# Small experts' up rows turned by plain transposes instead of half-merging products, and their second projections issued in one piece

## Chip, cores and metric

One core of a Trainium2 chip runs the whole program. The time is device microseconds of one launch; lower is better.

## What is computed

A two-layer decoder trunk on 256 tokens of width 1024: a retention layer with a dense SwiGLU, then a block-sparse attention layer with an eight-expert SwiGLU in which each token takes its top two experts. The change touches the expert part alone:

```python
def swiglu(x, w_in, w_out):
    gate, up = jnp.split(x @ w_in, 2, axis=-1)
    return (jax.nn.silu(gate) * up) @ w_out

def moe_swiglu(x, router, w_in, w_out):
    ...
    for e in range(N_EXPERTS):
        out = out + gates[:, e:e + 1].astype(x.dtype) * swiglu(xt, w_in[e], w_out[e])
```

Each expert has `w_in` of 1024 x 7168 and `w_out` of 3584 x 1024, all float32. The weights are read once.

## The kernel before

**Precision.** Matmuls run on 32-bit "fp32r" operands. Each weight tile is split in two parts, `whi` (a ScalarE copy that rounds, L894) and `wlo` (VectorE: the raw weights minus `whi`, L1056); each activation tile has such a pair as well. A product is then a sum of two or three matmuls.

**Units.** The expert weights come as units of 1 MB (128 x 2048). There are 8 jobs (one for each expert, sorted by how many tokens they have), each of 42 units. Four jobs are *big* (up to 128 tokens, three matmuls for each of four pieces: 12 matmuls of 512 columns for a unit, L1534 to L1536) and four are *small* (up to 64 tokens; the hi and lo halves of the 64 tokens lie side by side in the 128 columns of one stationary operand, so two matmuls for each piece: 8 for a unit, L1968 and L1969). Because of that, the result of a small gate or up product has 128 rows, 64 of the hi part and 64 of the lo part, and the two halves must still be added.

**Rings.** SyncE loads raw units into 8 buffers (`raw`, `more_raw`); a load is issued when the `wlo` of the unit eight places before is done. The split tiles `whi`/`wlo` have 4 buffers. In iteration n of its loop ScalarE writes `whi` of unit n + 4, for which it waits until TensorE has used unit n; VectorE then writes `wlo` of unit n + 4, and TensorE waits for that before unit n + 4.

**Order.** The order of the units is written out by hand in `STREAM`. A big and a small job run as a pair, in four blocks of the hidden dimension (4, 4, 4 and 2 units for each part). I call the place of a unit in its block, counted from the block's first unit (the big gate), its *offset*. Before, blocks 1 and 2 run: big gate (offsets 0 to 3), two units of small out of the block before (4, 5), big up (6 to 9), the other two of small out (10, 11), small gate (12 to 15), big out (16 to 19), small up (20 to 23). Block 0 of the second to fourth pair is the same with one and one unit of small out (22 units in all); block 3 has big gate 2, big up 2, small out 4, small gate 2, small up 2, big out 2. A pair is 84 units.

**Side work.** All of it is placed by unit number through tables such as `MUL_AT`, and lies between units in each engine's loop: of the big job, silu (ScalarE), times up (VectorE, L1424), transposes (TensorE, L1932), hi and lo of the turned rows (ScalarE L909, VectorE). Of the small job: ScalarE copies the gate rows to `rows4` (L918), TensorE turns them with eight 128 x 128 transposes (L2016), ScalarE copies the one half (L949), VectorE adds the other (L1452), ScalarE takes silu (L955). The up rows are copied too (L925), but they are turned by `turn_merged`: a product with `merge` (128 x 64, the sum of the identity's two halves), which turns the rows and adds the halves at once (L2006). VectorE multiplies straight from PSUM (L1458), ScalarE writes hi (L961), VectorE lo. Besides, four times in a pair a finished job's rows are split (`y_hi`, `y_lo`) and scattered by TensorE (L1902, L1903) and added to `h` (VectorE, L1415), and in the blocks of the first three pairs the next pair's tokens are gathered (L1871, copies L980 and L981).

Of the kernel before, what the change touches and what calls it, by code (L numbers as in the profile page):

```python
# [29 lines left out]
def build(nc, x, ln_g, ln_b, ret_w_in, ret_gn_g, ret_gn_b, ret_w_out, kv_w, moba_w_q, moba_w_out,  # L30
# [56 lines left out]
    for pair in range(JOBS // 2):  # L87
        for b in range(LAST + 1):
            big, small = 2 * pair, 2 * pair + 1
            end = pair == JOBS // 2 - 1 and b == LAST  # L90
            START[big, b] = len(STREAM)
            small_out = units_of(small, "out", b - 1) if b else units_of(small - 2, "out", LAST) if pair else []
            mid = len(small_out) // 2
            if b < LAST:
                STREAM += units_of(big, "gate", b) + small_out[:mid] + units_of(big, "up", b) + small_out[mid:]
                START[small, b] = len(STREAM)
                STREAM += units_of(small, "gate", b) + units_of(big, "out", b) + units_of(small, "up", b)
            else:
                STREAM += units_of(big, "gate", b) + units_of(big, "up", b) + small_out[:mid if end else None]
                START[small, b] = len(STREAM)  # L100
                STREAM += units_of(small, "gate", b) + units_of(small, "up", b) + units_of(big, "out", b)
            if end:
                STREAM += small_out[mid:] + units_of(small, "out", b)
# [23 lines left out]
    SEL_AT = {START[j - j % 2, 2] + 1 + 2 * (j % 2): j for j in range(JOBS)}  # L127
# [30 lines left out]
    with ctx:  # L158
# [59 lines left out]
        merge, _ = place("merge", [P, HALF])  # L218
# [33 lines left out]
        rows4, _ = place("rows4", [P, W], at=act4_at)  # L252
        act_small, _ = place("act_small", [P, BANK], at=past_at)
# [120 lines left out]
        gate_summed = sem("gate_summed")  # L374
        small_silu = sem("small_silu")
# [120 lines left out]
        def turned_gate():  # L496
            return ps[:, 0:2, :].rearrange("p a (c s n) -> p (a c) s n", s=2, n=HALF)
# [98 lines left out]
        def _(pool):  # L596
# [54 lines left out]
            pool.tensor_tensor(merge[:, :], ident[:, 0:HALF], ident[:, HALF:P], ALU.add).then_inc(moe_tables, 1)  # L651
# [7 lines left out]
            pool.wait_ge(moe_tables, 8)  # L659
# [24 lines left out]
        def _(act):  # L684
# [255 lines left out]

            def small_drains(n):

                if n in GATE_TURN_AT:
                    j, b = GATE_TURN_AT[n]
                    c = 2 * BLOCK_UNITS[b]
                    act.wait_ge(gate_turned, blocks(j, b))
                    if blocks(j, b) > 1:
                        act.wait_ge(small_lo, blocks(j, b) - 1)
                    nc.scalar.activation(act_small[:, 0:c * HALF].rearrange("p (c n) -> p c n", c=c),  # L949
                                         turned_gate()[:, 0:c, 1, :], ACT.Copy).then_inc(gate_half, 1)  # L950
# [42 lines left out]
            for n in range(MOE_UNITS):  # L993
# [4 lines left out]
                if n in SEL_AT:  # L998
                    copy_selT(SEL_AT[n], 3)
# [46 lines left out]
        def _(dve):  # L1046
# [316 lines left out]
            def sort_experts():  # L1363

                dve.wait_ge(counted, 1)
                dve.wait_ge(moe_tables, 9)
# [71 lines left out]
            def small_drains(n):  # L1438
# [8 lines left out]
                if n in GATE_SUM_AT:  # L1447
                    j, b = GATE_SUM_AT[n]
                    c = 2 * BLOCK_UNITS[b]
                    rows = act_small[:, 0:c * HALF].rearrange("p (c n) -> p c n", c=c)  # L1450
                    dve.wait_ge(gate_half, blocks(j, b))
                    nc.vector.tensor_tensor(rows, rows, turned_gate()[:, 0:c, 0, :], ALU.add).then_inc(gate_summed, 1)  # L1452
                if n in SMALL_MUL_AT:
                    j, b = SMALL_MUL_AT[n]
                    w = BLOCK_UNITS[b] * P
                    dve.wait_ge(small_silu, blocks(j, b))
                    dve.wait_ge(up_turned, blocks(j, b))
                    nc.vector.tensor_tensor(act_small[:, 0:w], act_small[:, 0:w], ps[:, 2, 0:w],  # L1458
# [72 lines left out]
        def _(pe):  # L1531
# [404 lines left out]
            def big_unit(n):  # L1936
# [10 lines left out]
                if q == 0 and part == "up" and blocks(j, b) > 1:  # L1947
                    pe.wait_ge(small_mul, blocks(j, b) - 1)
                    pe.wait_ge(up_copied, 7 * (j // 2) + 2 * b)
                    if b == 2:  # L1950
                        pe.wait_ge(selT_ready, j + 2)
# [19 lines left out]
            def small_unit(n):  # L1971
# [3 lines left out]
                if q == 0 and part == "gate":  # L1975
                    pe.wait_ge(big_silu, halves(j, b))
                    if b == 0:
# [25 lines left out]
            def turn_merged(rows, at, chunks):  # L2003

                for c in range(chunks):
                    last = pe.matmul(ps[:, at, c * HALF:(c + 1) * HALF], rows[:, c * P:(c + 1) * P], merge[:, :],  # L2006
                                     start=True, stop=True)
                return last

            def small_turn(n):  # L2010

                if n in GATE_TURN_AT:
                    j, b = GATE_TURN_AT[n]
                    pe.wait_ge(gate_copied, halves(j, b))
                    for c in range(2 * BLOCK_UNITS[b]):
                        last = pe.transpose(ps[:, c // 4, c % 4 * P:(c % 4 + 1) * P], rows4[:, c * P:(c + 1) * P], ident[:, :])  # L2016
                    last.then_inc(gate_turned, 1)
                if n in UP_TURN_AT:
                    j, b = UP_TURN_AT[n]
                    pe.wait_ge(up_copied, halves(j, b))  # L2020
                    turn_merged(rows4, 2, 2 * BLOCK_UNITS[b]).then_inc(up_turned, 1)
# [11 lines left out]
            pe.wait_ge(moe_tables, 9)  # L2033

            for n in range(MOE_UNITS):
# [19 lines left out]
                if n in SEL_AT:  # L2055
                    j = SEL_AT[n]
                    if SMALL[j]:
                        pe.wait_ge(selT_ready, j)
                    else:
                        pe.wait_ge(up_copied, 7 * (j // 2) + 4)  # L2060
                    turn_sel(sel_of(j), 3)
# [59 lines left out]
```

## Time and profile before

| what | value |
|---|---|
| three runs | 1403.58, 1406.47, 1406.56 us; median 1406.47 |
| the profiled execution | 1405.33 us, span of its records 1403.5 us |
| TensorE busy | 1371.3 us (98%) |
| VectorE busy | 1137.5 us (81%); in the expert part nearly all the time |
| ScalarE busy | 960.7 us (68%) |
| HBM read | 444.63 MB, 318 GB/s over the span |

The expert part runs from about 530 us to the end. Times in the trace are microseconds from the span's start; PE is TensorE, DVE VectorE, ACT ScalarE, SP SyncE. A duration is that of one instruction; where instructions overlap, the distance from one start to the next is shorter than the duration.

### The profile page before, as it was taken

To read this page: it belongs to the slowest core of one execution; us is meant where nothing else is said; L and a number is where in the kernel's file an instruction comes from. 1 tells how busy PE (TensorE), PEld (TensorE's weight loads), DVE (VectorE), ACT (ScalarE), POOL (GpSimd) and SP (SyncE) were. 2 spreads that over 40 slices of the span, in tenths; PEclk is the share of its full clock that TensorE was granted. 3 is DMA by queue.
4 is the path that set the end of the run, shared out by engine and by line. 5 is a ranking of instruction groups with operands and counts; after the bars stand their busy time and mean duration, and the time that the engine had idled before them with its cause. 6 is when DMAs were issued, how large, how long until landed. Compare 5 with 4: busy or idle time off the path is not lost.

```text
span 1403.5 us, 18365 instructions
## 1 busy us (share of the span) xinstructions
PE 1371.3 (98%) x7282; PEld 1172.3 (84%) x7282; DVE 1137.5 (81%) x807; ACT 960.7 (68%) x814; POOL 62.4 (4%) x64
## 2 busy tenths in 40 slices
PE   9999999999999999999999999999999999999996
PEld 9987788999979888788888788888788888788884
DVE  5455655444475668999999999999999999999997
ACT  5334444333454448788897888897888887888884
POOL 1001200000000003001100001200000000000000
PEclk9999999999999999999999999999999999999998
DMA  9654546555545437999999999999999999999992
GB/s 357 233 165 161 195 162 223 186 179 182 191 168 196 142 112 286 400 405 420 414 416 421 398 415 414 412 416 420 394 419 418 411 414 420 407 404 420 419 414 105
DMA packets 158742, 446.87 MB, mean 318 GB/s; under 512 B 7088, under 2 KB 46000, under 8 KB 158656
## 3 DMA queue, kind: packets, MB, share of 16 engines
q1 hardware_dynamic: 156832, 439.38, 80.9%
q0 software_dynamic: 1824, 6.33, 1.3%
q8 instruction: 56, 0.92, 0.2%
q14 instruction: 30, 0.25, 0.0%
HBM read 444.63 MB, written 1.05 MB: 318 GB/s over the span
## 4 chain that ended last, share of the span: by engine, by line
PE 81%; DVE 14%; ACT 2%; issue 2%; POOL 0%; DVEq 0%; ACTq 0%; POOLq 0%
PE ps L1534 20%; PE ps L1536 19%; PE ps L1535 19%; PE ps L1968 7%; PE ps L1969 7%; DVE wlo L1056 6%; DVE wlo_more L1056 3%; PE ps L2006 2%; PE ps L1871 1%; ACT whi L894 1%; DVE h L1415 1%; PE ps L1580 1%; PE ps L2016 1%; DVE wlo L431 1%; DVE act L1424 1%
## 5 line engine op out<-in xcount | busy, mean ns | idle before, releaser
L1056 DVE TENSOR_TENSOR wlo<-raw,whi 128x2048 fp32r<-128x2048 f32 (+1 forms) x214 | 478.8, 2256 | 16.8 <-ACT whi L894 16.6
L894 ACT ACTIVATE whi<-raw 128x2048 fp32r<-128x2048 f32 x208 | 395.3, 1916 | 69.6 <-PE ps L1536 66.0
L431 DVE TENSOR_TENSOR wlo<-raw,whi 128x2048 fp32r<-128x2048 f32 x80 | 183.5, 2294 | 155.2 <-ACT whi L424 155.2
L424 ACT ACTIVATE whi<-raw 128x2048 fp32r<-128x2048 f32 x82 | 156.8, 1912 | 153.3 <-PE ps L1536 150.4
L1534 PE MATMUL ps<-xT_hi,whi 128*128 128x256 f32 x576 | 163.4, 284 | 0.0
L1536 PE MATMUL ps<-xT_hi,wlo 128*128 128x256 f32 x576 | 163.0, 283 | 0.0
L1535 PE MATMUL ps<-xT_lo,whi 128*128 128x256 f32 x576 | 163.0, 283 | 0.0
L1534 PE MATMUL ps<-whi,xg_big 128*128 128x512 f32 x336 | 133.6, 398 | 2.0 <-DVE wlo L1056 2.0
L1968 PE MATMUL ps<-whi,xg_small 128*128 128x512 f32 x336 | 133.3, 397 | 0.0
L1536 PE MATMUL ps<-whi,xg_big 128*128 128x512 f32 x336 | 131.8, 392 | 0.0
L1535 PE MATMUL ps<-wlo,xg_big 128*128 128x512 f32 x336 | 131.4, 391 | 0.0
L1969 PE MATMUL ps<-wlo,xg_small 128*128 128x512 f32 x336 | 131.2, 391 | 0.0
L1534 PEld LDWEIGHTS ps<-xT_hi,whi 128*128 128x128 f32 x576 | 110.5, 192 | 0.5
L1535 PEld LDWEIGHTS ps<-xT_lo,whi 128*128 128x128 f32 x576 | 110.5, 192 | 0.4
L1536 PEld LDWEIGHTS ps<-xT_hi,wlo 128*128 128x128 f32 x576 | 110.5, 192 | 0.0
L1056 DVE TENSOR_TENSOR wlo_more<-raw,whi_more 128x2048 fp32r<-128x2048 f32 x42 | 96.0, 2285 | 3.2 <-ACT whi_more L894 3.2
L1056 DVE TENSOR_TENSOR wlo_more<-more_raw,whi_more 128x2048 fp32r<-128x2048 f32 x42 | 96.0, 2285 | 3.0 <-ACT whi_more L894 3.0
L1056 DVE TENSOR_TENSOR wlo<-more_raw,whi 128x2048 fp32r<-128x2048 f32 x42 | 96.0, 2286 | 2.7 <-ACT whi L894 2.7
L894 ACT ACTIVATE whi_more<-raw 128x2048 fp32r<-128x2048 f32 x42 | 80.6, 1920 | 10.7 <-PE ps L1536 10.7
L894 ACT ACTIVATE whi_more<-more_raw 128x2048 fp32r<-128x2048 f32 x42 | 80.6, 1920 | 10.5 <-PE ps L1536 10.5
L1534 PE MATMUL ps<-whi,xT_hi 128*128 128x512 f32 (+1 forms) x224 | 85.2, 380 | 2.4 <-DVE wlo L431 2.2
L894 ACT ACTIVATE whi<-more_raw 128x2048 fp32r<-128x2048 f32 x42 | 80.5, 1917 | 10.2 <-PE ps L1536 10.2
(273 smaller groups left out, 2686.4 us busy)
## 6 DMA issues: line engine op xcount, KB each, us to landing
raw<-in_moe_w_in SPq DMA_DIRECT2D x167, 1024.0 KB, 8.0
raw<-in_moe_w_out SPq DMA_DIRECT2D x85, 1024.0 KB, 8.3
more_raw<-in_moe_w_in SPq DMA_DIRECT2D x57, 1024.0 KB, 8.0
more_raw<-in_moe_w_out SPq DMA_DIRECT2D x27, 1024.0 KB, 8.5
raw<-in_ret_w_in SPq DMA_DIRECT2D x23, 1024.0 KB, 6.5
raw<-in_ffn_w_in SPq DMA_DIRECT2D x22, 1024.0 KB, 4.9
raw<-in_ffn_w_out SPq DMA_DIRECT2D x11, 1024.0 KB, 4.9
raw<-in_ret_w_out SPq DMA_DIRECT2D x8, 1024.0 KB, 4.8
```

What stands on the lines that cost most here:

```text
L424: nc.scalar.activation(whi[:, u % SPLIT, :], src, ACT.Copy).then_inc(hi_done, 1)
L431: nc.vector.tensor_tensor(wlo[:, u % SPLIT, :], src, whi[:, u % SPLIT, :].bitcast(F32), ALU.subtract).then_inc(lo_done, 1)
L894: nc.scalar.activation(moe_split(n)[0], moe_raw(n), ACT.Copy).then_inc(hi_done, 1)
L1056: return nc.vector.tensor_tensor(dst, src, hi.bitcast(F32), ALU.subtract)
L1415: nc.vector.scalar_tensor_tensor(out=h[:, t, :], in0=ps[:, at:at + 2, :].rearrange("p b n -> p (b n)"), scalar=gate, in1=h[:, t, :], op0=A ...
L1424: nc.vector.tensor_tensor(act4[:, cols], act4[:, cols], ps[:, 2 + half, :], ALU.mult).then_inc(big_mul, 1)
L1534: pe.matmul(dst, a_hi, b_hi, start=start, stop=False, skip_group_check=True)
L1535: pe.matmul(dst, a_hi, b_lo, start=False, stop=False, skip_group_check=True)
L1536: return pe.matmul(dst, a_lo, b_hi, start=False, stop=stop, skip_group_check=True)
L1968: pe.matmul(dst, a, hi, start=start, stop=False, skip_group_check=True)
L1969: return pe.matmul(dst, a, lo, start=False, stop=stop, skip_group_check=True)
L2006: last = pe.matmul(ps[:, at, c * HALF:(c + 1) * HALF], rows[:, c * P:(c + 1) * P], merge[:, :], start=True, stop=True)
```

## The change

The up rows of the small job are turned as the gate rows are, by plain transposes into two PSUM banks (2 and 3); a new ScalarE step copies the one half to `up_low` (it lies over `act4`), and VectorE adds the other half and multiplies afterwards, so its one step becomes two with a wait between them. The steps behind move: the multiplication from one to two units behind the small up part, hi from one to three, lo from two to four. The four units of small out that belong in a block come in one piece behind big up (offsets 8 to 11 in blocks 1 and 2; 8 and 9 in block 0). The two transposes of `sel` in block 2 move from offsets 1 and 3 to 5 and 7 and from bank 3 to bank 0. Table `merge` goes. The steps placed by the end of big up (`MUL_AT`, `TURN_AT`, `LO_AT`) move with it, two offsets earlier in blocks 1 and 2.

```diff
-            mid = len(small_out) // 2
             if b < LAST:
-                STREAM += units_of(big, "gate", b) + small_out[:mid] + units_of(big, "up", b) + small_out[mid:]
+                STREAM += units_of(big, "gate", b) + units_of(big, "up", b) + small_out
...
     UP_TURN_AT = {END[j, "up", b] + 1: (j, b) for j, b in SMALL_BLOCKS}
-    SMALL_MUL_AT = {END[j, "up", b] + 1: (j, b) for j, b in SMALL_BLOCKS}
-    SMALL_HI_AT = {END[j, "up", b] + 1: (j, b) for j, b in SMALL_BLOCKS}
-    SMALL_LO_AT = {END[j, "up", b] + 2: (j, b) for j, b in SMALL_BLOCKS}
+    UP_HALF_AT = {END[j, "up", b] + 1: (j, b) for j, b in SMALL_BLOCKS}
+    SMALL_MUL_AT = {END[j, "up", b] + 2: (j, b) for j, b in SMALL_BLOCKS}
+    SMALL_HI_AT = {END[j, "up", b] + 3: (j, b) for j, b in SMALL_BLOCKS}
+    SMALL_LO_AT = {END[j, "up", b] + 4: (j, b) for j, b in SMALL_BLOCKS}
...
-    SEL_AT = {START[j - j % 2, 2] + 1 + 2 * (j % 2): j for j in range(JOBS)}
+    SEL_AT = {START[j - j % 2, 2] + 5 + 2 * (j % 2): j for j in range(JOBS)}
...
                     if blocks(j, b) > 1:
-                        act.wait_ge(up_turned, blocks(j, b) - 1)
+                        act.wait_ge(small_mul, blocks(j, b) - 1)
                     silu_gate(half)
...
+                if n in UP_HALF_AT:
+                    j, b = UP_HALF_AT[n]
+                    c = 2 * BLOCK_UNITS[b]
+                    act.wait_ge(up_turned, blocks(j, b))
+                    nc.scalar.activation(up_low[:, 0:c * HALF].rearrange("p (c n) -> p c n", c=c),
+                                         turned_rows(2)[:, 0:c, 1, :], ACT.Copy).then_inc(up_half, 1)
...
                 if n in SMALL_MUL_AT:
...
+                    rows = up_low[:, 0:w].rearrange("p (c n) -> p c n", c=c)
+                    dve.wait_ge(up_half, blocks(j, b))
+                    then(nc.vector.tensor_tensor(rows, rows, turned_rows(2)[:, 0:c, 0, :], ALU.add))
                     dve.wait_ge(small_silu, blocks(j, b))
-                    dve.wait_ge(up_turned, blocks(j, b))
-                    nc.vector.tensor_tensor(act_small[:, 0:w], act_small[:, 0:w], ps[:, 2, 0:w],
+                    nc.vector.tensor_tensor(act_small[:, 0:w], act_small[:, 0:w], up_low[:, 0:w],
                                             ALU.mult).then_inc(small_mul, 1)
...
-            def turn_merged(rows, at, chunks):
+            def turn_rows(at, chunks):
 
                 for c in range(chunks):
-                    last = pe.matmul(ps[:, at, c * HALF:(c + 1) * HALF], rows[:, c * P:(c + 1) * P], merge[:, :],
-                                     start=True, stop=True)
+                    last = pe.transpose(ps[:, at + c // 4, c % 4 * P:(c % 4 + 1) * P], rows4[:, c * P:(c + 1) * P],
+                                        ident[:, :])
                 return last
```

`then` is a VectorE instruction followed by a wait of VectorE for its own result.

## Rows read from the trace of the kernel before

**Rows 1.** The page: busy us (share of the span) and instructions of each engine.

```profile
PE 1371.3 (98%) x7282; PEld 1172.3 (84%) x7282; DVE 1137.5 (81%) x807; ACT 960.7 (68%) x814; POOL 62.4 (4%) x64
```

**Rows 2.** Windows: busy time by engine, clock, DMA; blocks 0 to 3, second pair.

```profile
742.28:800.39 58.11, 56.72 (x258) 46.43 (x256) 57.69 (x38) 47.69 (x37) 0.00 (x0) 1.00 1.02 412
800.39:860.24 59.85, 59.85 (x285) 49.79 (x285) 57.99 (x32) 50.52 (x41) 0.00 (x0) 1.00 1.02 410
860.24:920.45 60.21, 60.21 (x289) 50.05 (x288) 57.81 (x32) 51.89 (x44) 11.55 (x4) 1.00 1.03 415
920.45:955.97 35.52, 35.52 (x177) 29.81 (x176) 35.09 (x20) 31.00 (x28) 0.00 (x0) 1.00 1.03 416
```

**Rows 3.** TensorE's waits from 600 us on: total us, times, longest us.

```profile
PE ps L1534 <- DVE wlo L1056: 3.3, 6, 0.7
```

**Rows 4.** The chain that ended last: start us, us, what.

```profile
844.07 0.87 PE ps L2016 x8
...
863.12 1.73 PE ps L2006 x16
```

**Rows 5.** Line L2006 and line L2016: duration ns min/median/max, first and last start.

```profile
L2006 PE MATMUL ps<-merge,rows x224: 217/275/275, 589.1 to 1374.5; 128*128 128x64 f32 x112
...
L2016 PE MATMUL ps<-ident,rows x112: 270/272/273, 570.1 to 1368.9; 128*128 128x128 f32 x112
```

**Rows 6.** Timeline of VectorE, block 1, second pair: start us, duration us, what.

```profile
827.68 2.29 DVE L1056 TENSOR_TENSOR wlo<-raw,whi 128x2048 fp32r<-128x2048 f32 x1 [0.43 <-ACT whi L894]
...
835.87 2.28 DVE L1056 TENSOR_TENSOR wlo_more<-more_raw,whi_more 128x2048 fp32r<-128x2048 f32 x1
838.07 0.68 DVE L1056 TENSOR_TENSOR gT_lo<-ps,gT_hi 128x512 fp32r<-128x512 f32 x1
838.67 2.28 DVE L1056 TENSOR_TENSOR wlo<-raw,whi 128x2048 fp32r<-128x2048 f32 x1
```

**Rows 7.** Timeline of ScalarE in the same block.

```profile
825.72 1.92 ACT L894 ACTIVATE whi<-raw 128x2048 fp32r<-128x2048 f32 x1 [0.80 <-PE ps L1536]
...
827.55 0.36 ACT L980 ACTIVATE xg_big<-ps 128x256 fp32r<-128x256 f32 x1
```

**Rows 8.** Timeline of TensorE: first matmuls at offsets 14, 15, 16 of that block.

```profile
837.32 0.40 PE L1968 MATMUL ps<-whi,xg_small 128*128 128x512 f32 x1
...
839.14 0.39 PE L1968 MATMUL ps<-whi_more,xg_small 128*128 128x512 f32 x1
...
841.10 0.47 PE L1534 MATMUL ps<-whi,gT_hi 128*128 128x512 f32 x1
```

**Rows 9.** Timeline of VectorE, first pair boundary: a long stretch, first and last row.

```profile
767.16 2.29 DVE L1056 TENSOR_TENSOR wlo<-raw,whi 128x2048 fp32r<-128x2048 f32 x1 [0.42 <-ACT whi L894]
...
797.96 4.48 DVE L1056 TENSOR_TENSOR wlo<-raw,whi 128x2048 fp32r<-128x2048 f32 x2
```

**Rows 10.** Group of ScalarE's half copy from 600 us on: busy us, mean ns.

```profile
L949 ACT ACTIVATE act_small<-ps 128x512 f32<-128x512 f32 x11 | 6.4, 578 | 0.0
```

**Rows 11.** Timelines of VectorE, then of TensorE, at the end.

```profile
1377.64 0.41 DVE L1458 TENSOR_TENSOR act_small<-act_small,ps 128x256 f32<-128x256 f32 x1
1377.97 2.28 DVE L1056 TENSOR_TENSOR wlo<-more_raw,whi 128x2048 fp32r<-128x2048 f32 x1
...
1382.71 1.28 DVE L1056 TENSOR_TENSOR y_lo<-ps,y_hi 128x512 fp32r<-128x512 f32 x2
...
1381.06 0.39 PE L1968 MATMUL ps<-whi,gT_last 128*128 128x512 f32 x1
...
1384.13 0.47 PE L1902 MATMUL ps<-y_hi,selT 128*128 128x512 f32 x1 [1.10 <-DVE y_lo L1056]
```

**Rows 12.** A late load's issue and landing, and ScalarE's start on it.

```profile
L562 SPq DMA_DIRECT2D more_raw<-in_moe_w_out x1: 373/373/373, 1361.0 to 1361.0; - x1
...
DMA to landing us min/median/max: 13.0/13.0/13.0
...
1374.03 1.92 ACT L894 ACTIVATE whi<-more_raw 128x2048 fp32r<-128x2048 f32 x1
```

More of the change, by code:

```diff
@@ L98, in build @@
             else:
-                STREAM += units_of(big, "gate", b) + units_of(big, "up", b) + small_out[:mid if end else None]
+                STREAM += units_of(big, "gate", b) + units_of(big, "up", b) + small_out[:2 if end else None]
                 START[small, b] = len(STREAM)
@@ L102, in build @@
             if end:
-                STREAM += small_out[mid:] + units_of(small, "out", b)
+                STREAM += small_out[2:] + units_of(small, "out", b)
     END = {(j, part, b): n for n, (j, part, b, q) in enumerate(STREAM)}
@@ L217, in build @@
         iota_twice, _ = place("iota_twice", [P, 2, HALF])
-        merge, _ = place("merge", [P, HALF])
         key_low, _ = place("key_low", [P, EX])
@@ L252, in build @@
         rows4, _ = place("rows4", [P, W], at=act4_at)
+        up_low, _ = place("up_low", [P, BANK], at=act4_at)
         act_small, _ = place("act_small", [P, BANK], at=past_at)
@@ L374, in build @@
         gate_summed = sem("gate_summed")
+        up_half = sem("up_half")
         small_silu = sem("small_silu")
@@ L494, in scatter_bank, with turned_rows @@
             return 2 if j == JOBS - 2 and t == 1 else 4 + 2 * (j % 2)
-        def turned_gate():
-            return ps[:, 0:2, :].rearrange("p a (c s n) -> p (a c) s n", s=2, n=HALF)
+        def turned_rows(at):
+            return ps[:, at:at + 2, :].rearrange("p a (c s n) -> p (a c) s n", s=2, n=HALF)
         def sel_of(j):
@@ L658, in _ @@
             pool.memset(key_limit[:, FIRST_SMALL:EX], float(EX * (HALF + 1))).then_inc(moe_tables, 1)
-            pool.wait_ge(moe_tables, 8)
+            pool.wait_ge(moe_tables, 7)
             pool.memset(key_low[:, 0:1], float(FIRST_KEY + EX - 1)).then_inc(moe_tables, 1)
@@ L998, in _ @@
                 if n in SEL_AT:
-                    copy_selT(SEL_AT[n], 3)
+                    copy_selT(SEL_AT[n], 0)
                 if n in (1, 5):
@@ L1365, in sort_experts @@
                 dve.wait_ge(counted, 1)
-                dve.wait_ge(moe_tables, 9)
+                dve.wait_ge(moe_tables, 8)
                 then(nc.vector.scalar_tensor_tensor(out=key[:, :], in0=ps[:, 2, EX:2 * EX], scalar=float(EX),
@@ L1451, in small_drains @@
                     dve.wait_ge(gate_half, blocks(j, b))
-                    nc.vector.tensor_tensor(rows, rows, turned_gate()[:, 0:c, 0, :], ALU.add).then_inc(gate_summed, 1)
+                    nc.vector.tensor_tensor(rows, rows, turned_rows(0)[:, 0:c, 0, :], ALU.add).then_inc(gate_summed, 1)
                 if n in SMALL_MUL_AT:
@@ L1976, in small_unit @@
                     pe.wait_ge(big_silu, halves(j, b))
+                    if b == 2:
+                        pe.wait_ge(selT_ready, j + 1)
                     if b == 0:
@@ L2014, in small_turn @@
                     pe.wait_ge(gate_copied, halves(j, b))
-                    for c in range(2 * BLOCK_UNITS[b]):
-                        last = pe.transpose(ps[:, c // 4, c % 4 * P:(c % 4 + 1) * P], rows4[:, c * P:(c + 1) * P], ident[:, :])
-                    last.then_inc(gate_turned, 1)
+                    turn_rows(0, 2 * BLOCK_UNITS[b]).then_inc(gate_turned, 1)
                 if n in UP_TURN_AT:
@@ L2020, in small_turn @@
                     pe.wait_ge(up_copied, halves(j, b))
-                    turn_merged(rows4, 2, 2 * BLOCK_UNITS[b]).then_inc(up_turned, 1)
+                    turn_rows(2, 2 * BLOCK_UNITS[b]).then_inc(up_turned, 1)
             warm_up(ROUTER_WARM[3], 6)
@@ L2032, in _ @@
             last.then_inc(counted, 1)
-            pe.wait_ge(moe_tables, 9)
+            pe.wait_ge(moe_tables, 8)
             for n in range(MOE_UNITS):
@@ L2056, in _ @@
                     j = SEL_AT[n]
+                    pe.wait_ge(big_silu, 7 * (j // 2) + 5)
                     if SMALL[j]:
                         pe.wait_ge(selT_ready, j)
-                    else:
-                        pe.wait_ge(up_copied, 7 * (j // 2) + 4)
-                    turn_sel(sel_of(j), 3)
+                    turn_sel(sel_of(j), 0)
                 if n in GATHER_AT:
```

6 lines of the change are left out of this document (2 added, 4 removed).

## The prediction

> **What bounds the kernel now.** I read the page first: TensorE is busy 98% of the span [rows 1], and so is the chain of waits, which runs over its matmuls for most of its length. That average doesn't say how near the others are. The windows of one pair of jobs do: in 213.69 us (58.11 + 59.85 + 60.21 + 35.52) TensorE idles only in block 0, by 1.39 us; VectorE is busy for 57.69, 57.99, 57.81 and 35.09 us; and the transfers run at 410 to 416 GB/s [rows 2]. So three resources stand close together, and a gain on TensorE counts only where VectorE and the loads follow.
>
> VectorE's busy time needs care. One `wlo` lasts 2.28 us but the next instruction begins 2.20 us after its start, and a 512-column step of 0.68 us gives way after 0.60 [rows 6]. I count starts: 84 x 2.20, and for the side work of a pair 7 + 7 + 4 steps of 0.6, four additions of 1.2, nine full and three half steps for the small job, some 22 in all: 207 us of 213.7.
>
> Where does that bind? A big unit (12 matmuls) takes TensorE 2.72 us, a small one (8) 1.82 [rows 8], and VectorE needs 2.20 for either. VectorE gains ground beside big units and loses it beside small ones. What it can gain is bounded by the ring: `whi` of unit n + 4 starts when unit n is used (0.1 after), takes 1.92, and `wlo` starts 0.04 behind it [rows 7, 6]. At the end of the six small units of block 1 the lead is just gone: the last one should take 1.82 and takes 1.96 [rows 8], a wait of 0.14, of the kind of which the list of waits shows little (3.3 us in all) [rows 3].
>
> **The turn.** Eight plain transposes take 0.87 us, the 16 instructions of eight merging products 1.73 [rows 4]; each product is two records where a transpose is one [rows 5]. So 0.87 us of TensorE goes away behind each of the twelve four-unit small up parts (blocks 0 to 2, four pairs: 10.4 us) and 0.4 behind each two-unit one (three pairs: 1.2; that of the last pair lies in the tail, below). **Gain at most 11.6 us.**
>
> The pages weigh in on this. The Trainium skill, TensorE: Matmul & The Clock Gate, section "Part 4: PE-mode transpose", gives a transpose some 275 ns in the context of a kernel. The duration of a row agrees (272 ns) [rows 5], but starts here lie 0.11 us apart (0.87 / 8), and the sum goes by starts.
>
> **The new steps.** ScalarE gets one copy of 0.58 [rows 10] for each block, VectorE one addition; of the same form and size as the gate's, so 0.6. The trace before has no wait of VectorE for itself in this place; it costs at least the 0.08 by which a duration exceeds its distance, and at most some 0.2, if a semaphore needs another 0.1 as ScalarE's copies do behind TensorE. I take 0.1: 0.7 us a block on VectorE, 2.3 us a pair (the half-size one 0.4). They stand in iterations 0 and 1 of a block, beside big units, where VectorE still waits for ScalarE (0.43 before a `wlo`) [rows 6]; cost 0 there. If that cover were gone, 2.3 us a pair. Counted with the same distances, the multiplication is done 9.9 us into the block, and the big up part, which waits for it, starts at 11.9 (four units of 2.72, the turn, the refill); small out, which waits for lo (done at 15), starts at 23. No new wait there. ScalarE loses its wait for the multiplication, which costs nothing now.
>
> **Eight small units in a row.** This is the price. I set T = 0 at the end of big up. TensorE alone reaches big out (offset 16) after 8 x 1.82 + two transposes of 0.44, and in the first three pairs two gathers of 0.43, with 0.13 lost to refill behind each transposing: 16.65 us; in the last pair, without gathers, 15.7. VectorE cannot begin the fourth `wlo` of the run (offset 11) before 0.1 + 1.92 + 0.04 = 2.06; then come six `wlo` (13.2), one times-up and two lo steps (1.8) up to that of offset 16: 17.06, and TensorE starts 0.15 later, at 17.2. Wait: 0.55 in block 1, 1.5 in the last pair. The same count for the present order, with only four `wlo`, one times-up and one lo from the end of big up at offset 9, gives 12.2 against 12.03, 0.17, and the trace shows 0.14: the method holds. In block 2 the second `sel` transposing (0.44) falls on TensorE's side of the run, and its ScalarE copy (0.37) pushes the gather copies (0.36 and more [rows 7]) and through them VectorE by 0.3: waits of 0.3 and 1.1. More waiting than before: 3 x 0.41 + 3 x 0.16 + 1.35 + 0.93 = **4.0 us**.
>
> The bounds: nothing, if VectorE keeps its lead, and 1.4 in each of the eight runs, if the gathers don't help as in the last pair (11.2 - 1.2 = 10 us).
>
> **Block 0** of pairs two to four. VectorE works without a break from 767.16 to the end of the `wlo` of the next block's first unit (33 us) [rows 9], and TensorE waits for that. Now big up ends one offset earlier by count but 0.91 later by time (a big unit instead of a small one ahead of it), one times-up (0.6) falls into VectorE's wait before the stretch, and the stretch started 0.1 to 0.2 late before: about +0.1 each, **0.3 us**. Its start and end don't gain from the turn, which lies in the next block's first unit.
>
> **The tail.** The last small out waits for lo of the last block, which moves from two to four units behind small up. Today VectorE multiplies at 1377.64, is on the next `wlo` at 1377.97, and the last out starts at 1381.06; TensorE then waits anyway, to 1384.13, for `y_lo`, which VectorE starts at 1382.71 [rows 11]. New order on VectorE: `wlo` to 1379.8, addition and multiplication to 1380.6, last `wlo` to 1382.8, `y_lo` to 1384.0, and only then lo of the small job, 1384.4. The last out but one starts at 1384.5 instead of 1381.06; behind it come a unit of 1.82, a scatter of 0.91 and the last unit, so that TensorE is through at 1389.1 instead of 1387.0: **+2.1 us**, and nothing behind it hides that.
>
> **The loads.** They give a unit in about 2.49 us (1.049 MB at 421 GB/s, a little over the means of rows 2), 209 us a pair; my new pair takes 211.4. They keep up, but at the very end there is no reserve: the load issued at 1361.0 takes 13.0 us, and ScalarE starts on it at 1374.03, the moment it lands [rows 12]. I add **0.3 us**, between 0 and the 3 us that the last pairs could want it earlier.
>
> **Sum.** -11.6 + 4.0 + 0.3 + 2.1 + 0.3 = -4.9 us. The profiled execution took 1405.33 us (span 1403.5 and 1.8 around it), 1.1 under the median of the three runs. So 1400.4 for such an execution, and against the median, 1406.47: **1401.6 us**, 0.35% faster.
>
> **Rivals.**
> - *VectorE keeps its lead in the runs* (no more waiting than now): -8.9, 1397.6 us. For it speaks that the wait list is nearly empty today; against it, that six small units in a row already use up the lead. 0.13.
> - *All eight runs starve as in the last pair*: +6 to the sum, 1407.6, no change. The gathers are 0.86 us of cover that a late ScalarE copy can spoil. 0.19.
> - *The loads take half of the gain*: 1404. For it: rows 12, and a floor of 209 of 211.4; against it, that they have pauses today when all eight buffers are full. 0.10.
> - *VectorE becomes the bound, slower*: the place is the `wlo` of offset 16, in each of the eight runs. All else sums to -8.9 (11.6 less the tail, block 0 and the loads), and the eight runs wait 1.2 us in all now: so the point from which it decides is a mean wait of 1.3 us a run, and over 0.2% slower begins at 1.6. At 2.0 us a run (the added 0.7 us of VectorE work arriving late in the run too) it is 16 - 1.2 - 8.9 = +5.9: 1412.4 us. For it: VectorE at 58 of 59.85 us. 0.10. The Trainium skill, VectorE: DVE Perf Modes, section "The DRAIN you can't avoid", speaks for this rival: the next instruction does not start until the pipe is empty, and one should keep the number of operations small. By that each `wlo` would hold VectorE for its whole 2.28 us, and a run would wait 0.6 us longer; the starts 2.20 apart [rows 6] disagree, so the chance is not raised.
> - *The turn gives nothing*: if a transpose held TensorE for its duration (0.272 x 8 = 2.2 us against 1.73), the gain of 11.6 would become a loss of 6: 1419. Rows 4 say otherwise. 0.01.
> - The forecast: 0.47, its own range 1399 to 1404.
>
> **Chances.** 0.2% (2.8 us) is about what a measurement of this kernel can tell from no change. Faster: most of the forecast (0.38), the first rival (0.13), half of the loads (0.05), some of the starving (0.03): 0.59. Slower: the fourth and fifth, and a little of the second: 0.13. Same: 0.28. The range takes in the first rival's bound and the second's: 1397 to 1408.
>
> **What would show it.** Right: no L2006 of 16 but transposes of 0.87 at a block's start; a wait of TensorE for `wlo` of 0.3 to 0.6 us before big out in blocks 1 and 2 of the first three pairs, and over 1 us in the last; the last small out starting 3 us later relative to the last `wlo`; VectorE's pair at 209 us of start distances. Wrong: waits of over 1.3 us in all runs, a wait of the big up part for the multiplication, a TensorE wait for a gather copy behind offset 9 above 0.5 us, or `whi` waiting for loads through the last pair.

## The result, and the profile after

The changed kernel takes **1443.68 us** (median of 4 runs, 1439.65 to 1449.61) against 1406.47 (1403.58 to 1406.56): 1.0264 times the time before, 95% interval 1.0233 to 1.0295. That is 37 us slower, where 5 us faster was forecast, and far outside the range. The profiled execution took 1439.65 us with a span of 1437.8, 34.3 us more than before.

The page of the kernel after: busy us (share of the span) and instructions, then the granted clock in 40 slices of the span.

```profile
PE 1375.8 (96%) x7170; PEld 1166.3 (81%) x7170; DVE 1145.9 (80%) x823; ACT 971.1 (68%) x830; POOL 53.3 (4%) x63
...
PEclk9999999999999999999999999999999999999997
```

TensorE is busy 4.5 us longer than in [rows 1] although it executes 112 records fewer, and it idles 30 us more. Busy time that grows while work goes away is the first hint: some instructions last longer. The clock row hides it, since no slice but the last falls under 0.9. The windows of the four blocks of the second pair, the stretches of [rows 2], show where:

```profile
748.55:807.04 58.49, 56.71 (x257) 46.42 (x256) 58.21 (x39) 47.35 (x35) 0.00 (x0) 1.00 1.01 386
807.04:866.88 59.84, 59.33 (x276) 48.79 (x277) 58.50 (x33) 51.97 (x43) 0.00 (x0) 1.00 1.02 415
866.88:926.98 60.10, 59.74 (x281) 49.05 (x280) 58.23 (x33) 52.59 (x45) 7.21 (x4) 1.00 1.03 416
926.98:970.43 43.45, 37.94 (x166) 30.75 (x164) 35.76 (x21) 31.97 (x30) 0.00 (x0) 0.92 0.96 366
```

Blocks 0 to 2 are as long as before within 0.4 us. Block 3 takes 43.45 us instead of 35.52, TensorE idles 5.5 us in it where it idled none, and its granted clock is 0.92. The distances between the first matmuls of successive blocks give the same picture over all four pairs (us; the last entry runs to the end of the last small out unit):

```
        pair 1                    pair 2                    pair 3                    pair 4
before  58.09 60.06 60.28 35.52   58.10 59.85 60.21 35.52   58.11 59.83 60.29 35.53   58.11 59.04 59.41 40.84
after   56.51 60.25 60.07 43.45   58.49 59.84 60.10 43.45   58.50 59.81 59.99 43.45   58.49 59.47 59.61 51.42
```

Block 3 is 7.93 us longer three times and 10.6 in the last pair, where the tail is in it: 34.4 us, all of the difference. (Nothing was changed in the first block and in the dense part ahead of it, and yet over the traces of this document the one varies by 1.9 us and the other by 7. That is why blocks are compared below and not only totals.)

TensorE's waits in the list of waits of after, from 540 us on (us in total, times, longest us):

```profile
PE ps L1543 <- DVE act_small L1467: 12.5, 4, 3.1
PE ps L1975 <- DVE gT_small L1062: 10.1, 4, 2.9
...
PE ps L1975 <- DVE gT_last L1062: 3.5, 1, 3.5
PE ps L1975 <- DVE wlo_more L1062: 3.0, 7, 0.7
```

The two waits on top are new. Each comes four times, once in each block 3: TensorE's big up part waits 3.1 us for the multiplication (L1467), and small out 2.4 us for lo of the rows (`gT_small`, L1062; 2.9 in the last pair, where no gather stands ahead of it). The waits for `wlo_more`, which the prediction priced as the whole cost, are the small fourth row. Windows through the head of block 3, second pair, say what happens around them:

```profile
930.50:933.50 3.00, 3.00 (x15) 2.15 (x13) 3.00 (x3) 1.91 (x2) 0.00 (x0) 1.00 1.04 409
933.50:936.60 3.10, 0.01 (x1) 0.00 (x0) 3.07 (x4) 1.91 (x1) 0.00 (x0) 1.00 1.05 407
936.62:941.10 4.48, 4.48 (x13) 3.56 (x14) 2.14 (x1) 0.60 (x1) 0.00 (x0) 0.62 1.06 411
941.06:943.80 2.74, 2.74 (x13) 2.25 (x12) 0.53 (x1) 2.43 (x2) 0.00 (x0) 1.00 1.04 422
943.80:946.80 3.00, 0.61 (x5) 0.41 (x3) 3.00 (x4) 2.35 (x3) 0.00 (x0) 1.00 0.94 367
946.80:949.70 2.90, 2.88 (x8) 2.29 (x9) 2.16 (x1) 0.00 (x0) 0.00 (x0) 0.65 0.97 329
949.70:953.00 3.30, 3.30 (x17) 2.75 (x16) 1.05 (x1) 2.46 (x2) 0.00 (x0) 0.79 0.93 312
```

Rows two and five are the waits (row five has a gather of 0.6 us ahead of its wait). Rows three, six and seven show the third cost: having stood for 3.1 and 2.4 us, TensorE works at a granted clock of 0.62 to 0.79, so part of the time at the lower of its two levels, 1.2 GHz instead of 2.4. The unit at 936.62 lasts 4.44 us; the same unit lasts 2.90 where the wait is filled and the clock stays up (e8 below). The last pair differs: behind a first wait that is just as long, its clock stayed up.

```profile
1379.39:1382.28 2.89, 2.89 (x12) 2.36 (x13) 2.14 (x1) 0.60 (x1) 0.00 (x0) 1.00 1.05 415
```

Why does the multiplication come late? VectorE's timeline over the same place (start us, duration us, what, wait before it):

```profile
930.75 2.28 DVE L1062 TENSOR_TENSOR wlo_more<-raw,whi_more 128x2048 fp32r<-128x2048 f32 x1
932.96 2.28 DVE L1062 TENSOR_TENSOR wlo<-raw,whi 128x2048 fp32r<-128x2048 f32 x1
935.16 0.68 DVE L1465 TENSOR_TENSOR up_low<-up_low,ps 128x512 f32<-128x512 f32 x1
935.87 0.69 DVE L1467 TENSOR_TENSOR act_small<-act_small,up_low 128x512 f32<-128x512 f32 x1
936.48 2.28 DVE L1062 TENSOR_TENSOR wlo<-raw,whi 128x2048 fp32r<-128x2048 f32 x1
943.27 2.29 DVE L1062 TENSOR_TENSOR wlo<-more_raw,whi 128x2048 fp32r<-128x2048 f32 x1 [4.50 <-ACT whi L894]
945.48 0.68 DVE L1430 TENSOR_TENSOR act<-act,ps 128x512 f32<-128x512 f32 x1
946.08 0.68 DVE L1062 TENSOR_TENSOR gT_small<-act_small,gT_small 128x512 fp32r<-128x512 f32 x1
```

VectorE never waits for the new addition's inputs. It does the addition and the multiplication where its order puts them, behind the splitting of two more units (930.75 and 932.96), for which nobody is in a hurry: those units are used at 941.06 and 946.82. TensorE stands from 933.5 on, behind the gate part of block 3, which has only two units. Its first matmul behind the wait:

```profile
936.62 0.50 PE L1543 MATMUL ps<-whi,xg_big 128*128 128x512 f32 x1 [3.10 <-DVE act_small L1467]
```

And ScalarE, which shows where the second wait comes from:

```profile
941.32 1.92 ACT L894 ACTIVATE whi<-more_raw 128x2048 fp32r<-128x2048 f32 x1 [4.06 <-PE ps L1545]
943.14 0.61 ACT L967 ACTIVATE gT_small<-act_small 128x512 fp32r<-128x512 f32 x1
```

The split buffer of `whi` at 941.32 comes free only when TensorE has finished the unit at offset 2; `wlo` at 943.27 waits 4.50 us for that `whi`; lo of the rows (946.08) stands behind that `wlo` and a times-up; and TensorE's small out, two units behind the one at offset 2, needs lo. From the end of that unit (941.06) to small out (946.82) this takes 5.76 us, and TensorE has 3.35 us of work for it. So the second wait comes from the place of lo in the queue and not from the first wait: where the first is cut to 0.9 us (e2) or filled (e8), the second is as long as before.

The sum for a block 3, from the distances between the starts of its units in the second pair (us):

```
unit      0     1     2     3     4     5    12   the others
before  4.42  2.85  2.72  3.14  1.85  2.68  3.60  14.26
after   3.52  6.11  4.45  5.75  2.89  3.35  3.08  14.29
```

Units 0 and 12 hold the two turns: -0.90 and -0.52. Units 1 and 3 end with the waits: +3.26 and +2.61. Units 2, 4 and 5 stand behind them: +1.73, +1.04 and +0.67; with the clock at 1.00 the same three take 2.90, 1.93 and 2.68 (e8), so 3.2 of these 3.44 us are clock. Together 7.9, as measured; about 40% of it is clock.

### The profile page after: what moved, and what is told of

Its sections match the earlier page's. It is cut to its first block, busy times and chain, and to the rows that moved or that the text cites. A ratio compares the mean times of both kernels' runs of the same rounds, so it can differ in the third digit from the quotient of the medians.

```text
span 1437.8 us, 18176 instructions
## 1 busy us (share of the span) xinstructions
PE 1375.8 (96%) x7170; PEld 1166.3 (81%) x7170; DVE 1145.9 (80%) x823; ACT 971.1 (68%) x830; POOL 53.3 (4%) x63
## 4 chain that ended last, share of the span: by engine, by line
PE 71%; DVE 21%; ACT 4%; issue 3%; POOL 0%; DVEq 0%; ACTq 0%; POOLq 0%
PE ps L1543 19%; PE ps L1545 19%; PE ps L1544 19%; DVE wlo L1062 11%; DVE wlo_more L1062 4%; PE ps L1975 4%; PE ps L1976 4%; ACT whi L894 1%; ACT whi_more L894 1%; PE ps L2015 1%; DVE act L1430 1%; DVE gT_lo L1062 1%; PE ps L1880 1%; PE ps L1589 1%; DVE wlo L432 1%
## 5 line engine op out<-in xcount | busy, mean ns | idle before, releaser
L1062 DVE TENSOR_TENSOR wlo<-raw,whi 128x2048 fp32r<-128x2048 f32 (+1 forms) x214 | 477.7, 2255 | 32.5 <-ACT whi L894 31.9
L1543 PE MATMUL ps<-whi,xg_big 128*128 128x512 f32 x336 | 135.7, 404 | 12.6 <-DVE act_small L1467 12.5
L1545 PE MATMUL ps<-whi,xg_big 128*128 128x512 f32 x336 | 133.3, 397 | 0.0
L1062 DVE TENSOR_TENSOR wlo<-more_raw,whi 128x2048 fp32r<-128x2048 f32 x42 | 95.9, 2284 | 9.3 <-ACT whi L894 9.3
L1062 DVE TENSOR_TENSOR wlo_more<-raw,whi_more 128x2048 fp32r<-128x2048 f32 x42 | 95.9, 2284 | 2.9 <-ACT whi_more L894 2.7
L1062 DVE TENSOR_TENSOR wlo_more<-more_raw,whi_more 128x2048 fp32r<-128x2048 f32 x42 | 95.9, 2284 | 2.7 <-ACT whi_more L894 2.6
L1543 PEld LDWEIGHTS ps<-whi,xg_big 128*128 128x128 f32 x336 | 64.3, 191 | 28.3 <-DVE act_small L1467 14.2
```

The source lines that it names most:

```text
L1062: return nc.vector.tensor_tensor(dst, src, hi.bitcast(F32), ALU.subtract)
L1543: pe.matmul(dst, a_hi, b_hi, start=start, stop=False, skip_group_check=True)
L1545: return pe.matmul(dst, a_lo, b_hi, start=False, stop=stop, skip_group_check=True)
```

## The experiments

Block lengths of experiments come from their traces in the way of the table above. Each ratio is to the kernel before, run on the same chip (its medians there were 1405.85, 1406.62 and 1406.60).

**e1, the new order alone.** The kernel before with the new order of units; the turn stays merged, all steps at the old offsets.

```
-                STREAM += gate + small_out[:mid] + up + small_out[mid:]
+                STREAM += gate + up + small_out
```

> The kernel before with the new order of units alone (small out in one piece behind big up); the merging products and all steps stay as they were. Theory S (the loss comes from where the steps behind small up are placed, and shows in block 3): block 3 stays at 35.5 us; blocks 1 and 2 pay for eight small units in a row, about 0.9 us each, 8 of them, so +7 us: 1413 us. Rival R (the run of eight starves VectorE and is the loss): most of the 37 us come back here, 1435 to 1445. Rival W (the added ScalarE copy and VectorE addition are the loss): near 1407.

Measured: 1431.51 us, 1.0175 (1.0127 to 1.0224). The total seems to blame the order, but the blocks don't: block 3 is 35.53 us in the first three pairs and 40.86 in the last, the values of before. Most of the loss sits in block 2 (64.2, 64.5, 65.9, 63.8 us):

```profile
PE ps L1533 <- ACT selT L966: 11.2, 4, 2.8
```

The big up part now starts at offset 4 and waits for a copy of `sel` that is turned at offset 3. The change moves that turning (`SEL_AT`), this kernel does not: a fault of the experiment, mended in e7. Behind this wait of 2.8 us the clock fell in the third pair (0.61, the unit there takes 4.41 us) and stayed up in the other three (2.8 us each). What e1 does show: the order without the new steps leaves block 3 alone.

**e2, multiplication one offset earlier**, **e3, hi and lo one offset earlier**, **e4, both.** In the kernel after, as short diffs:

```
e2, e4
-    SMALL_MUL_AT = {END[j, "up", b] + 2: ...}
+    SMALL_MUL_AT = {END[j, "up", b] + 1: ...}
e3, e4
-    SMALL_HI_AT = {END[j, "up", b] + 3: ...}
-    SMALL_LO_AT = {END[j, "up", b] + 4: ...}
+    SMALL_HI_AT = {END[j, "up", b] + 2: ...}
+    SMALL_LO_AT = {END[j, "up", b] + 3: ...}
```

> The changed kernel with the small job's addition and multiplication one unit earlier (END + 1); hi and lo stay at +3 and +4. Theory S: in block 3 the wait of big up at offset 2 falls from 3.1 us to about 0.8 and TensorE keeps its clock there (1.7 us); the wait of small out at offset 4 stays. 4 us for each of four blocks 3: 1443.7 - 16 = 1428 us. Rival W: the same work in the same amount, so the time stays within 3 us of 1443.

Measured: 1424.15 us, 1.0127 (1.0078 to 1.0176). Block 3 takes 39.63, 39.65 and 38.06 us. The list of waits of e2:

```profile
PE ps L1975 <- DVE gT_small L1062: 10.2, 4, 2.9
...
PE ps L1543 <- DVE act_small L1467: 3.7, 4, 0.9
```

> The changed kernel with the small job's hi at +2 and lo at +3 (they were at +3 and +4); addition and multiplication stay at +2. Theory S: lo no longer stands behind the wlo of offset 6, which needs big up's first unit to be used, so the wait of small out at offset 4 in block 3 (2.9 us, with 1.5 to 2 us of lost clock and drained ring behind it) goes, and the tail gets 2 us back; the wait of big up at offset 2 stays. 1443.7 - 20 = 1424 us. Rival W: within 3 us of 1443.

Measured: 1426.59 us, 1.0135 (1.0088 to 1.0183). Block 3 takes 39.21, 39.23 and 40.28 us. Here `act_small` keeps its 12.5 us and `gT_small` is gone from the list.

> The changed kernel with both: addition and multiplication at +1, hi at +2, lo at +3. Theory S: block 3 falls from 43.5 us to 35 or 36, the last pair's from 51.4 to 42; the whole comes back to 1408 us, give or take 4. Rival W: still 1435 or more. Rival R: still over 1425.

Measured: 1412.34 us (10 runs), 1.0050 (1.0028 to 1.0073); block 3 takes 35.37, 35.37 and 35.39 us. Its list of waits:

```profile
PE ps L1975 <- DVE gT_last L1062: 3.7, 1, 3.7
PE ps L1543 <- DVE act_small L1467: 3.7, 4, 0.9
```

Three numbers in the tables of offsets give back 31 of the 37 us, with the same instructions on every engine. In the second pair each half saves about 4 us of block 3 (3.8 and 4.2), and both together 8.1. (In the third pair it is 5.4 and 3.2: behind e2's second wait the clock stayed up there, in e3 it was down for longer.) The place of the new steps costs block 3 8 us; the steps as such use up its gain from the two turns (1.4 us by the table of units, 0.15 left), mostly through the wait of 0.9. What e4 still loses against before lies in the last block (44.83 us against 40.84), in block 0 (0.4 three times) and behind the last small out (0.9).

**e5, the turn alone.** The order of before, with the plain turn and e4's offsets; for block 3's up rows hi and lo are one offset earlier still (+1 and +2).

```
-                STREAM += gate + up + small_out
+                STREAM += gate + small_out[:mid] + up + small_out[mid:]
```

> The turn alone: units in the order of the kernel before, plain transposes, half copy and addition as in the change, but the steps early: addition and multiplication at +1, hi at +2, lo at +3 (in block 3, +1 and +2 as before); sel as in the change. Theory S: blocks 1 and 2 gain the turn (0.87 us each, 59.85 to 59.1 and 60.2 to 59.3), block 3 gains less, since big up at its offset 2 still waits 0.9 us for the multiplication; the last block as before, 41 us. 1406.5 - 7 = 1399 us. Rival W (the added ScalarE and VectorE steps eat the gain wherever they stand): 1405 to 1409.

Measured: 1407.90 us, 1.0002 (0.9979 to 1.0026). The gain of 0.87 a block does not arrive. In the order of before small out stands at offset 4 of blocks 1 and 2, and now waits for lo:

```profile
PE ps L1976 <- DVE gT_small L1063: 5.1, 8, 0.8
PE ps L1912 <- DVE y_lo L1063: 4.6, 4, 1.4
PE ps L1544 <- DVE act_small L1468: 4.0, 4, 1.0
```

Eight times up to 0.8: the chain half copy, addition, multiplication, hi, lo is longer than the merged one and eats what the turn freed.

**e6, a mixed turn.** As e5, but plain only for the up rows of blocks 0 and 1, whose turns lie in the heads of blocks 1 and 2; merged for blocks 2 and 3.

```
+    PLAIN = 2
-    UP_HALF_AT = {END[j, "up", b] + 1: (j, b) for j, b in SMALL_BLOCKS}
+    UP_HALF_AT = {END[j, "up", b] + 1: (j, b) for j, b in SMALL_BLOCKS if b < PLAIN}
```

> As the kernel before in order and steps, but the up rows of blocks 0 and 1 alone are turned by plain transposes (their turns stand in blocks 1 and 2, which have four units of big gate to hide the longer chain); blocks 2 and 3 keep the merging product. Theory S: blocks 1 and 2 each gain up to 0.87 us, block 3 stays at 35.5: 1406.5 - 6.5 = 1400 us. Rival W: 1405 to 1409.

Measured: 1406.76 us, 1.0003 (0.9981 to 1.0026). Blocks 1 and 2 of the second pair stay at 59.98 and 60.19 with the same eight waits for `gT_small` (5.1 us). Block 0 is back at 58.10, from 58.47 in e5: the plain turn of the last two blocks costs block 0 its 0.37.

**e7, the new order done fairly.** e1 with the turning of `sel` and its bank moved as in the change.

```
-    SEL_AT = {START[j - j % 2, 2] + 1 + 2 * (j % 2): j for j in range(JOBS)}
+    SEL_AT = {START[j - j % 2, 2] + 5 + 2 * (j % 2): j for j in range(JOBS)}
```

> The kernel before with the new order and the new place and bank of the sel transposes; merging products and steps as before. It is the first experiment without its flaw (there big up in block 2 waited for the copy of sel). Blocks 0, 1 and 2 at 58.5, 60.75 and about 61 us, block 3 at 35.5: +0.9 us for each run of eight and +0.4 in block 0, 8.5 in all: 1415 us. If the run of eight were the loss, 1430 or more.

Measured: 1415.52 us, 1.0064 (1.0033 to 1.0095). Second pair: 58.50, 60.78, 61.00, 35.54. Blocks 1 and 2 are 0.6 to 1.4 us longer than before, 7.1 us over the eight, block 0 0.4. So the new order costs 8 to 9 us in all, not 37, and block 3 nothing.

**e8, the wait filled.** The kernel after with 26 transposes of the identity, written to a free bank and read by nobody, in front of the big up part of block 3. They occupy TensorE for 3.0 of the 3.1 us for which it stood.

```
+                if STREAM[n][1:] == ("gate", LAST, 1) and not SMALL[STREAM[n][0]]:
+                    for _ in range(26):
+                        pe.transpose(ps[:, 1, 0:P], ident[:, :], ident[:, :])
```

> The changed kernel with 26 transposes of the identity, some 2.8 us, put into TensorE's wait before big up in block 3 (they go to bank 1, and nothing reads them). They tell what the lower clock behind the wait costs apart from the wait: if it is the clock that stretches big up's first unit from 2.7 to 4.4 us, that unit falls to 2.8 and the granted clock there stays at 1.00: 1.6 us for each block 3, 1443.7 - 6.5 = 1437 us. If the unit is slow for another reason, nothing changes or the time rises by up to 1 us.

Measured: 1433.68 us, 1.0193 (1.0154 to 1.0231), 10 us less than after, with 104 transposes more. Windows of e8, second pair: the filling, the first up unit behind it, and the first two small out units:

```profile
934.66:937.92 3.26, 3.00 (x27) 2.75 (x25) 3.23 (x4) 1.92 (x1) 0.00 (x0) 1.00 1.05 408
937.92:940.82 2.90, 2.90 (x13) 2.36 (x13) 2.15 (x1) 0.60 (x1) 0.00 (x0) 1.00 1.05 408
946.57:948.50 1.93, 1.93 (x8) 1.61 (x9) 1.93 (x1) 0.00 (x0) 0.00 (x0) 1.00 1.01 410
948.50:951.19 2.69, 2.69 (x18) 2.32 (x16) 0.70 (x2) 2.43 (x2) 0.00 (x0) 1.00 0.98 361
```

All at 1.00. But this is one pair. Block 3 takes 41.84, 40.31, 40.25 and 51.32 us, so it is 1.6, 3.1, 3.2 and 0.1 us shorter than in after, 8.05 in all. The first up unit behind the filling takes 2.9 us at 1.00 in every pair, as expected; that gives back 1.56 us in each of the first three (in the last, the clock had not fallen there in after). The rest was not expected: behind the second wait, which is as long as ever (`gT_small` 10.2 us), the clock stayed up in pairs 2 and 3. In pairs 1 and 4 it fell:

```profile
726.25:728.83 2.58, 2.58 (x9) 2.03 (x10) 2.14 (x1) 0.00 (x0) 0.00 (x0) 0.73 1.01 408
1383.06:1386.46 3.40, 3.40 (x9) 2.69 (x9) 2.15 (x1) 0.00 (x0) 0.00 (x0) 0.53 1.02 418
```

In e2, with a first wait of 0.9 us, it stayed up behind the second in one pair of four. So the filling is shown to save the clock behind the wait that it fills; whether it did anything for the second is not shown.

**e9, small out in pairs.** e5's steps, block 0 in the order of before, and in blocks 1 and 2 two up units, two small out, two up, two small out. Small out then starts at offset 6 and no more than six small units stand in a row.

```
+                STREAM += gate + ups[:2] + small_out[:2] + ups[2:] + small_out[2:]
```

> The turn with early steps, and in blocks 1 and 2 the order big gate 4, big up 2, small out 2, big up 2, small out 2: the first small out stands at offset 6 instead of 4, and the run of small units stays at six. Theory L (in the experiment with the turn alone, TensorE reached small out at offset 4 earlier by the faster turn and waited there for lo, 5.1 us in eight waits, so the gain only changed its place): that wait is gone and blocks 1 and 2 take 59.1 and 59.4 us instead of 60.0 and 60.2: 1406.5 - 6 = 1400 us. Rival D (VectorE as a whole sets the pace of these blocks, wherever TensorE waits): 60 us each, and 1406 to 1408 in all.

Measured: **1402.34 us** (10 runs), 0.9967 (0.9946 to 0.9987), faster than both kernels (than the one before by 0.3%). Second pair: 58.42, 58.95, 59.38, 35.38. Blocks 1 and 2 keep the turn: 0.9 and 0.8 us in this pair, 6.5 over the eight. TensorE idled nowhere in these blocks before [rows 2], so the order alone had next to nothing to give; it was not run with the merging turn. No `gT_small` is left in the waits:

```profile
PE ps L1916 <- DVE y_lo L1067: 4.6, 4, 1.4
PE ps L1548 <- DVE wlo L1067: 4.1, 6, 0.8
PE ps L1548 <- DVE act_small L1472: 3.9, 4, 1.0
```

**e10, alternating unit by unit**: e9 with one up, one small out, and so on.

```
+                STREAM += gate + [u for both in zip(ups, small_out) for u in both]
```

> As the last, but big up and small out alternate unit by unit in blocks 1 and 2 (first small out at offset 5, the run of small units is five long: one out and four gate). Theory L: as the last and without the wait before big out (0.15 each): blocks 1 and 2 at 59.0 and 59.3, 1399.5 us. Rival D: 60 us each, 1406 to 1408.

Measured: 1404.50 us, 0.9993 (0.9977 to 1.0009). Blocks 1 and 2 take 59.53 and 59.91 in the three pairs with gathers, 0.6 more than expected, and 58.03 and 58.42 in the last, without them. The row that is new is TensorE's wait for the gather's copies:

```profile
PE ps L1885 <- ACT xg_small L992: 1.9, 6, 0.3
```

That is 0.3 of the 0.6 us; the other half was not traced further.

**e11, the tail alone.** The kernel after with the steps of block 3's small up at the offsets of before, all others as after.

```
-    SMALL_MUL_AT = {END[j, "up", b] + 2: ...}
+    SMALL_MUL_AT = {END[j, "up", b] + (1 if b == LAST else 2): ...}
```

(and in the same way 1 for hi and 2 for lo)

> The changed kernel with the steps of block 3's small up alone at their old places (multiplication and hi at +1, lo at +2); all others stay late. The prediction's tail step: the last block comes back by 3 to 4 us (from 51.4 to 47.5), its wait of 3.5 us for lo before the last small out is gone; blocks 3 of the other pairs stay at 43.4. 1443.7 - 3.5 = 1440 us. If the tail were late because of the loads or VectorE's backlog, the last block stays over 50 us.

Measured: 1439.13 us, 1.0255 (1.0221 to 1.0288). The first three blocks 3 stay at 43.4, since their waits come from block 2's steps. The last goes from 51.42 to 48.09: the tail's price was 3.3 us.

**e12, mixed turn and alternating order.** e6 with e10's order.

> Plain transposes for the up rows of blocks 0 and 1 alone, merging products for blocks 2 and 3 with their old steps, and big up and small out alternating in blocks 1 and 2. Theory L: blocks 0 and 3 as before the change (58.1, 35.5, last block 40.9), blocks 1 and 2 at 59.0 and 59.3: 1406.5 - 7 = 1399.5 us, clear of the kernel before. Rival D: 1406.

Measured: 1403.14 us (12 runs), 0.9982 (0.9964 to 0.9999). Second pair: 58.11, 59.51, 59.97, 35.56. It is as fast as e9 within the intervals. The mixed turn with e9's order wasn't tried.

## Why the prediction was wrong

**The step that failed** is in "The new steps": "the multiplication is done 9.9 us into the block, and the big up part, which waits for it, starts at 11.9 (four units of 2.72, the turn, the refill); small out, which waits for lo (done at 15), starts at 23. No new wait there." This is true of blocks 1 and 2, and the list of waits shows none there. Block 3 has two gate units. Its big up part is at offset 2 and its small out at offset 4. END is the unit ahead of the block, so END + 2 and END + 4 are offsets 1 and 3: each step is queued just one unit before its reader, and in VectorE's queue the `wlo` of a unit three places further on stands ahead of it. The same arithmetic, applied to block 3, would have given it: after the turn the gate part is over at about 6.5 us (933.5 - 926.98), the multiplication at 9.6, a wait of 3. It wasn't applied: the new steps were worked out for the long blocks only, and their wait in block 3 was put at nothing.

Shown by e2, e3 and e4: each step moved by one offset takes away its own wait (the first down to 0.9 us), and both together bring block 3 from 43.45 to 35.4. The rivals named waits in the run of eight, the loads, VectorE's total and the transposes; none named this one. "A wait of the big up part for the multiplication" stood only under what would show the forecast wrong, without a price. That the work itself costs the time is refuted by e4 and e9, which do all of it.

**The clock** was in no term. The prediction priced waits as their length. Behind the two waits of a block 3 the units took 3.2 us more than at the full clock, 3.2 of the 7.9 us in each of the first three pairs; in the last it was 1.6, behind the second wait alone.

**The turn** (gain at most 11.6): right by its size. TensorE's chain in after has turns of 0.87 where it had 1.73, and e9's blocks 1 and 2 are 6.5 us shorter over the eight.

**The run of eight** (4.0 us): the right mechanism, undersized. By e7 it costs 7.1 us over the eight blocks. The last pair came as counted (1.38 and 1.10 against 1.35 and 0.93). In the others it was 0.6 to 0.9 and 0.7 to 0.8 instead of 0.41 and 0.16. In block 1 of the second pair big out starts 17.46 us after the end of big up:

```profile
830.28 0.39 PE L1975 MATMUL ps<-whi,gT_small 128*128 128x512 f32 x1
...
847.74 0.47 PE L1543 MATMUL ps<-whi,gT_hi 128*128 128x512 f32 x1 [0.18 <-DVE wlo L1062]
```

The count had 17.2. VectorE was 0.25 later than counted. And TensorE's own work was shorter than assumed: by the unit starts, the same units between the gate part and big out took 27.88 us before, 27.74 without the wait of 0.14, and take 28.80 now, so that the wait is 1.06 in all where the count had 0.55. Some 0.5 us, if it is so in all six blocks, is the missing 3 us. They ate the turn exactly: blocks 1 and 2 of after are as long as before (59.84 against 59.85).

**Block 0** (0.1 each): 0.4 each. TensorE's wait for `y_lo` in it grows from 0.73 us to 1.72, of which 0.6 comes back at the block's last unit. In after the order brings all of it: e7, with the merging turn, has the same wait of 1.72 and the same 58.50. In the old order the plain turn alone brings 0.37 (e5 against e6).

**The tail** (2.1 us): mechanism right, mis-sized at 3.3. VectorE did what was foreseen, `y_lo` and only then lo:

```profile
1410.88 2.28 DVE L1062 TENSOR_TENSOR wlo_more<-more_raw,whi_more 128x2048 fp32r<-128x2048 f32 x1
1413.08 1.28 DVE L1062 TENSOR_TENSOR y_lo<-ps,y_hi 128x512 fp32r<-128x512 f32 x2
1414.28 0.41 DVE L1062 TENSOR_TENSOR gT_last<-act_small,gT_last 128x256 fp32r<-128x256 f32 x1
```

The wait for lo is 3.5, and one of 1.4 for `y_lo`, which e11 has in its place, falls away: 2.1, as predicted. The rest is clock again, as TensorE's timeline shows:

```profile
1414.75 0.50 PE L1975 MATMUL ps<-whi,gT_last 128*128 128x512 f32 x1 [3.47 <-DVE gT_last L1062]
...
1415.73 0.63 PE L1976 MATMUL ps<-wlo,gT_last 128*128 128x512 f32 x1
1416.16 0.63 PE L1975 MATMUL ps<-whi,gT_last 128*128 128x512 f32 x1
```

Matmuls start 0.43 apart instead of 0.23; the unit takes 3.12 us (to 1417.87) instead of 1.82.

**The new steps' own price** (VectorE's wait for its own result at 0.1): right. The multiplication starts 0.71 behind the addition (935.16, 935.87), where 0.60 is the distance without a wait. VectorE's starts in after lie 2.20 apart at durations of 2.28 (930.75, 932.96, 935.16). The fourth rival read the Trainium skill too shortly here: VectorE: DVE Perf Modes, section "The DRAIN you can't avoid", says in the same place that a next operation that is not held starts earlier. With that the trace agrees, and the section did not speak for the rival.

**The loads** (0.3 us): they were no bound in after, since everything was slower; in block 3 they fell to 366 GB/s while the ring stood. In e9 nothing points to them either: by the traces blocks 1 and 2 give 6.5 us, block 0 takes 1.0, block 3 0.5 and the stretch behind the last small out 0.9, which leaves 4.1 of the measured 4.3.

## What to carry to other kernels

A step that is given a place relative to the end of a part ("two units after up") must be counted against its consumer in every kind of block, the shortest first: there the same offset is nearer to the reader. In a kernel whose engines take their work in a fixed order, a small operation costs what stands ahead of it in the queue and not its own 0.6 us, so put it one unit earlier before asking whether it is too expensive. A gain of TensorE time is kept only if the order leaves VectorE room to follow: here the turn's gain in blocks 1 and 2 arrived only when the small units were spread (e9).

## What the hardware showed

- A wait of TensorE of 2.4 to 3.1 us can cost more than its length. Behind the first wait of block 3 in after (3.1 us) the granted clock was 0.62 over the next 4.4 us in three pairs and 1.00 in the fourth; behind the second (2.4 us, in the fourth pair 2.9) it was 0.65, 0.65, 0.68 and 0.52 over the next unit. TensorE had been busy for 59.74 of the 60.10 us of the block before. Behind e1's four waits of 2.8 us the clock fell once. What decides it is not shown. Where it fell, the units behind took some 1.6 us more. Behind waits of 0.9 us (e4) and 1.7 us (block 0 of after) it stayed at 1.00.
- The Trainium skill, TensorE: Matmul & The Clock Gate, section "Part 4: PE-mode transpose", says that the full clock doesn't engage in transpose mode. The measurement differs: through 26 fp32 transposes in a row, 3.0 us, the granted clock was 1.00, and in all four pairs the unit behind them took 2.9 us (in after 4.4 in three pairs and 2.9 in one). The clock was full when they began: they kept it, and whether they could raise it no run shows.
- Useless work in a wait made the kernel 10 us faster by the medians (e8; 8 by the blocks of its trace). Taking both waits away made it 31 us faster (e4).
